# Experts of 112 token rows a pass in place of 128, with three passes behind the branch

## The reference

```python
def moe_swiglu(xn, w_router, w_gu, w_down):
    logits = (xn @ w_router).astype(jnp.float32)
    vals, idx = lax.top_k(logits, TOP_K)              # 2 of 8
    wts = jax.nn.softmax(vals, axis=-1)
    combine = jnp.sum(jax.nn.one_hot(idx, N_EXPERTS, dtype=jnp.float32) * wts[..., None], axis=-2).astype(xn.dtype)
    out = jnp.zeros_like(xn)
    for e in range(N_EXPERTS):
        out = out + combine[..., e:e + 1] * swiglu(xn, w_gu[e], w_down[e])
    return out
```

## Time and profile before

| | |
|---|---|
| median of 3 runs | 1527.17 us (1526.97 to 1527.71) |
| profiled execution, span from first to last instruction | 1525.5 us |
| mean granted TensorE clock | 0.996 |
| PE busy | 1492.0 us (98%) |
| PEld busy | 1214.1 us (80%) |
| DVE busy | 1187.4 us (78%) |
| ACT busy | 986.0 us (65%) |
| POOL busy | 57.1 us (4%) |
| DMA | 455.57 MB, mean 299 GB/s |

### The profile page before, as it was taken

The page is one execution under the profiler, slowest core; times in us unless marked ns, Lnnn a source line. Parts: engine busy times, 40 slices in busy tenths (PEclk is TensorE's granted clock), DMA queues, the critical chain, the costliest instruction groups (busy, mean ns, idle before and its releaser), DMA issues.

```text
span 1525.5 us, 20065 instructions
## 1 busy us (share of the span) xinstructions
PE 1492.0 (98%) x7081; PEld 1214.1 (80%) x7081; DVE 1187.4 (78%) x1047; ACT 986.0 (65%) x1001; POOL 57.1 (4%) x83
## 2 busy tenths in 40 slices
PE   7999999999999989999999999999999999999998
PEld 6888788887776568888888888888888888888886
DVE  1489655545658558898888889889888889888997
ACT  4645444444525527778777778778778778778774
POOL 2000100000111010000000000000000000000100
PEclk9999999999999989999999999999999999999999
DMA  9333585448638039999999999999999999999994
GB/s 363 130 111 111 185 257 180 178 166 220 217 138 290 15 110 374 369 363 386 394 367 377 394 378 363 393 391 355 395 376 362 395 385 357 393 392 356 397 392 169
DMA packets 213026, 455.57 MB, mean 299 GB/s; under 512 B 9857, under 2 KB 36522, under 8 KB 212970
## 3 DMA queue, kind: packets, MB, share of 16 engines
q1 hardware_dynamic: 206624, 441.48, 79.8%
q0 software_dynamic: 3536, 12.96, 2.1%
q10 hardware_dynamic: 2810, 0.40, 0.2%
HBM read 434.89 MB, written 19.92 MB: 298 GB/s over the span
## 4 chain that ended last, share of the span: by engine, by line
PE 94%; DVE 4%; POOL 1%; issue 1%; ACT 0%; DMA 0%; DVEq 0%; POOLq 0%; ACTq 0%
PE bank L2354 60%; PE bank L1947 8%; PE bank L1964 4%; PE bank L1817 4%; PE bank L1858 3%; PE bank L2033 2%; PE bank L2209 2%; PE bank L1839 2%; PE bank L2374 2%; PE bank L1891 1%; PE bank L2103 1%; PE bank L2067 1%; DVE small L1517 1%; PE bank L2151 1%; PE bank L2178 1%
## 5 line engine op out<-in xcount | busy, mean ns | idle before, releaser
L1676 DVE TENSOR_TENSOR w_lo<-ring,w_hi 128x2048 fp32r<-128x2048 f32 x333 | 756.4, 2290 | 104.6 <-ACT w_hi L1027 104.0
L1027 ACT ACTIVATE w_hi<-ring 128x2048 fp32r<-128x2048 f32 x333 | 638.0, 1920 | 168.8 <-PE bank L2354 168.6
L2354 PE MATMUL bank<-w_hi,x_hi 128*128 128x512 f32 x896 | 244.3, 394 | 0.7 <-DVE x_lo L1684 0.7
L2354 PE MATMUL bank<-w_hi,x_lo 128*128 128x512 f32 x896 | 240.0, 390 | 0.0
L2354 PE MATMUL bank<-w_lo,x_hi 128*128 128x512 f32 x896 | 239.7, 389 | 0.0
L2354 PEld LDWEIGHTS bank<-w_hi,x_lo 128*128 128x128 f32 x896 | 168.2, 188 | 35.9
L2354 PEld LDWEIGHTS bank<-w_lo,x_hi 128*128 128x128 f32 x896 | 168.2, 188 | 35.2
L2354 PEld LDWEIGHTS bank<-w_hi,x_hi 128*128 128x128 f32 x896 | 164.5, 188 | 32.3 <-issue 0.9
L1241 DVE TENSOR_TENSOR ring_lo<-ring,f_whi 128x1024 fp32r<-128x1024 f32 x66 | 80.6, 1225 | 75.5 <-ACT f_whi L817 75.5
L2354 PE MATMUL bank<-w_hi,t_hi 128*128 128x512 f32 x448 | 122.6, 395 | 0.0
L2354 PE MATMUL bank<-w_hi,t_lo 128*128 128x512 f32 x448 | 121.1, 392 | 0.0
(11 more groups left out here) (307 smaller groups left out, 1596.6 us busy)
## 6 DMA issues: line engine op xcount, KB each, us to landing
ring<-in_moe_w_gu SPq DMA_DIRECT2D x224, 1024.0 KB, 7.6
ring<-in_moe_w_down SPq DMA_DIRECT2D x112, 1024.0 KB, 8.1
ring<-in_ffn_w_gu SPq DMA_DIRECT2D x22, 1024.0 KB, 8.1
ring<-in_hgrn_w_in SPq DMA_DIRECT2D x16, 1024.0 KB, 15.2
ring<-in_ffn_w_down SPq DMA_DIRECT2D x10, 1024.0 KB, 6.3
x_rows<-arena SPq DMA_DIRECT2D x2, 4096.0 KB, 20.2
ring<-in_kv_w SPq DMA_DIRECT2D x6, 1024.0 KB, 6.3
ring<-in_hgrn_w_out SPq DMA_DIRECT2D x4, 1024.0 KB, 6.3
```

What stands on the lines that cost most here:

```text
L1027: act.activation(w_hi[s % PARTS][:, :], raw[:, s % RAWS, :], ACT.Copy).then_inc(hi_ready, 1)
L1676: dve.tensor_tensor(w_lo[s % PARTS][:, :], raw[:, s % RAWS, :], w_hi[s % PARTS][:, :].bitcast(F32), ALU.subtract).then_inc(lo_ready, 1)
L2354: last = mm(out_, x_[k], w[:, k, 512 * b:512 * b + 512], start=start and k == 0 and n == 0, stop=stop and k == HALF // width - 1 and n == 2)
```

## The change

`CAP = 112` takes the place of `P = 128` wherever a tile or a matmul has a token row of an expert as a partition or a column, and `PASSES = 3` passes cover 256 rows at most (3 x 112 = 336). The scratch has 336 rows an expert instead of 256. The branch is taken at more than 112 rows of an expert, and then two further passes run instead of one. The zero fill covers all 2688 rows of `x_rows` and 2 x 112 rows of each expert in `y_rows`, in six DMAs of SP's instead of four; the waits for it go to 96. The core of the diff:

```diff
-ROWS = 2 * P
+CAP, PASSES = 112, 3
+ROWS = PASSES * CAP
...
                 sp.dma_start(x_rows.rearrange("(n p) c -> p n c", p=P)[:, :, 512 * a:512 * a + 512],
-                             b_zero.unsqueeze(1).broadcast_to([P, 2 * NE, 512])).then_inc(x_zero, 16)
-                sp.dma_start(y_rows.rearrange("(n q p) c -> q p n c", q=2, p=P)[1, :, :, 512 * a:512 * a + 512],
-                             b_zero.unsqueeze(1).broadcast_to([P, NE, 512])).then_inc(x_zero, 16)
+                             b_zero.unsqueeze(1).broadcast_to([P, NE * ROWS // P, 512])).then_inc(x_zero, 16)
+                for q in range(1, PASSES):
+                    sp.dma_start(y_rows.rearrange("(n q p) c -> q p n c", q=PASSES, p=CAP)[q, :, :, 512 * a:512 * a + 512],
+                                 b_zero[0:CAP, :].unsqueeze(1).broadcast_to([CAP, NE, 512])).then_inc(x_zero, 16)
...
-            with sp.If(most > P):
-                all_experts(NE)
+            with sp.If(most > CAP):
+                for q in range(1, PASSES):
+                    all_experts(q * NE)
...
-                    pool.dma_start(m_xg, rows(x_rows, e + 1, q)).then_inc(x_full, 16)
+                    pool.dma_start(m_xg[0:CAP, :], rows(x_rows, e + 1, q)).then_inc(x_full, 16)
...
-                    last = act.activation(x_hi[:, k, :], bank[:, b, P * (k % 4):P * (k % 4) + P], ACT.Copy,
+                    last = act.activation(x_hi[:, k, 0:CAP], bank[:, b, P * (k % 4):P * (k % 4) + CAP], ACT.Copy,
...
-                act.activation(t_hi[:, c % 2, :, :], bank[:, 4, :], ACT.Copy).then_inc(t_hi_ok, 1)
+                act.activation(t_hi[:, c % 2, :, 0:CAP], bank[:, 4, :].rearrange("p (b t) -> p b t", b=4)[:, :, 0:CAP],
+                               ACT.Copy).then_inc(t_hi_ok, 1)
...
-            dve.wait_ge(x_zero, 64)
+            dve.wait_ge(x_zero, 96)
...
-                                  m_P[:, tb, :], start=tb == 0, stop=tb == 1)
+                                  m_P[:, tb, 0:CAP], start=tb == 0, stop=tb == 1)
...
-                    last = tp(bank[:, b, P * (k % 4):P * (k % 4) + P], m_xg[:, P * k:P * k + P], ident)
+                    last = tp(bank[:, b, P * (k % 4):P * (k % 4) + CAP], m_xg[0:CAP, P * k:P * k + P], ident[0:CAP, 0:CAP])
...
-                    product([bank[:, 2 * (c % 2) + up, :]], 2 * gu_item(c, up) + a, E,
-                            [x_hi[:, k, :] for k in ks], [x_lo[:, k, :] for k in ks], 512, a == 0, a == 1)
+                    product([bank[0:CAP, 2 * (c % 2) + up, :]], 2 * gu_item(c, up) + a, E,
+                            [x_hi[:, k, 0:CAP] for k in ks], [x_lo[:, k, 0:CAP] for k in ks], 512, a == 0, a == 1)
...
-                    last = tp(bank[:, 4, P * b:P * b + P], m_h[:, c % 2, P * b:P * b + P], ident)
+                    last = tp(bank[:, 4, P * b:P * b + CAP], m_h[0:CAP, c % 2, P * b:P * b + P], ident[0:CAP, 0:CAP])
...
-                    product([bank[:, 5, :], bank[:, 6, :]], 2 * down_item(c) + a, E,
-                            [t_hi[:, c % 2, b, :] for b in bs], [t_lo[:, c % 2, b, :] for b in bs], D,
+                    product([bank[0:CAP, 5, :], bank[0:CAP, 6, :]], 2 * down_item(c) + a, E,
+                            [t_hi[:, c % 2, b, 0:CAP] for b in bs], [t_lo[:, c % 2, b, 0:CAP] for b in bs], D,
```

More of the change, by code:

```diff
@@ L630, in rows @@
             def rows(block, e, q):
-                return block[bass.ds(e * ROWS + q * P, P), :]
+                return block[bass.ds(e * ROWS + q * CAP, CAP), :]
             def stored(e, E, q):
-                pool.wait_ge(y_ready, E + (2 + q))
-                pool.dma_start(rows(y_rows, e, q), m_y).then_inc(y_out, 16)
+                pool.wait_ge(y_ready, E + (2 + min(q, 1)))
+                pool.dma_start(rows(y_rows, e, q), m_y[0:CAP, :]).then_inc(y_out, 16)
             def brought():
@@ L650, in all_experts @@
                     pool.wait_ge(x_ps, 2 * E0)
-                    pool.dma_start(m_xg, rows(x_rows, 0, q)).then_inc(x_full, 16)
+                    pool.dma_start(m_xg[0:CAP, :], rows(x_rows, 0, q)).then_inc(x_full, 16)
                 with pool.Fori(0, NE - 1) as e:
@@ L659, in all_experts @@
                 pool.wait_ge(y_out, 16 * (E0 + NE))
-            pool.wait_ge(x_zero, 64)
+            pool.wait_ge(x_zero, 96)
             pool.wait_ge(y_out, 16)
@@ L674, in _ @@
             most = pool.value_load(flag[0:1, 0:1], min_val=0, max_val=T)
-            with pool.If(most > P):
-                all_experts(NE, 1)
+            with pool.If(most > CAP):
+                for q in range(1, PASSES):
+                    all_experts(q * NE, q)
                 pool.wait_ge(mixed, 1)
@@ L1050, in expert @@
                         act.wait_ge(e_h, E * NCH + (c - 1))
-                    act.activation(m_sl[:, c % 2, :], bank[:, 2 * (c % 2), :], ACT.Silu).then_inc(e_sl, 1)
+                    act.activation(m_sl[0:CAP, c % 2, :], bank[0:CAP, 2 * (c % 2), :], ACT.Silu).then_inc(e_sl, 1)
                     if c:
@@ L1056, in expert @@
                         act.wait_ge(PT_ps, 1)
-                        act.activation(m_PT[:, :], bank[:, 7, 0:T], ACT.Copy).then_inc(PT_ready, 1)
+                        act.activation(m_PT[0:CAP, :], bank[0:CAP, 7, 0:T], ACT.Copy).then_inc(PT_ready, 1)
                 split_to(min(2 * gu_item(NCH - 1, 1) + 1 + PARTS, HALVES + ahead), E)
@@ L1074, in expert @@
                             act.wait_ge(*used(HALVES - 1, E))
-                        act.activation(m_y[:, 512 * half:512 * half + 512], bank[:, 5 + half, :], ACT.Copy).then_inc(y_ready, 1)
+                        act.activation(m_y[0:CAP, 512 * half:512 * half + 512], bank[0:CAP, 5 + half, :], ACT.Copy).then_inc(y_ready, 1)
                 else:
-                    act.activation(m_y[:, :], bank[:, 5:7, :].rearrange("p b n -> p (b n)"), ACT.Copy).then_inc(y_ready, 1)
+                    act.activation(m_y[0:CAP, :], bank[0:CAP, 5:7, :].rearrange("p b n -> p (b n)"), ACT.Copy).then_inc(y_ready, 1)
                 splits[0] = ahead
@@ L1093, in _ @@
             most = act.value_load(flag[0:1, 0:1], min_val=0, max_val=T)
-            with act.If(most > P):
+            with act.If(most > CAP):
                 act.wait_ge(sc_ps, 4)
-                all_experts(NE, 1)
+                for q in range(1, PASSES):
+                    all_experts(q * NE, q)
         @block.vector
@@ L1763, in _ @@
             most = dve.value_load(flag[0:1, 0:1], min_val=0, max_val=T)
-            with dve.If(most > P):
+            with dve.If(most > CAP):
                 dve.memset(small[:, 505:506], 0.0).then_inc(mixed, 1)
-                all_experts(NE, 1)
+                for q in range(1, PASSES):
+                    all_experts(q * NE, q)
                 for tb in range(TB):
@@ L2441, in _ @@
             most = pe.value_load(flag[0:1, 0:1], min_val=0, max_val=T)
-            with pe.If(most > P):
-                all_experts(NE, 1)
+            with pe.If(most > CAP):
+                for q in range(1, PASSES):
+                    all_experts(q * NE, q)
 _INS = ["x", "norm_mix", "norm_ffn", "hgrn_w_in", "hgrn_w_out", "hgrn_g_norm", "kv_norm", "kv_w",
```

27 lines of the change are left out of this document (13 added, 14 removed).

## The result

The changed kernel takes 1549.28 us (median of 4 runs, 1548.69 to 1549.45) against 1527.18 for the kernel before on the same chip: a ratio of 1.0146, interval 1.0133 to 1.0158. It is slower by 22.1 us, where a gain of 3.8 us was forecast. The profiled execution has a span of 1547.8 us, against 1525.5 before.

The account below looks back on a forecast made before the run. PE was taken to bound the expert stage. Transposes -3.7 and first gather -0.1, all else zero, gave -3.8 us, so 1523.4 us; the forecast's own range was 1522.5 to 1525.3, the overall range 1516.5 to 1528.0.

Parts of the forecast that it names:

- What bounds the kernel, and the branch: Expert stage: PE sets the pace, DMA and DVE close behind; largest expert count 102 is below 112, so no extra pass.
- Zero fill: Scratch zeroing on SP's queue: 5.8 MB more at 384 GB/s takes 15 us, landing at 450.3; cost 0, bounds 0 and 2 us.
- the cover: Slack before the zero fill's landing delays DVE at line 1470: 1.8 us, and 3.3 us until the chain would move.
- rival E: Zero fill lands late enough to make the kernel slower; 3 us net needs 5.8 MB at 230 GB/s; chance 0.02.
- Products: The 4032 expert product matmuls: shorter load, 188 to 174 ns, gains zero; 6 us less or 2 us more allowed.
- the excess of 11 to 12 ns: Product pitch of 228 ns against 216 at line 1817, claimed to come from streaming 512 float32r columns, not the load.
- Transposes: 280 transposes in `turn` and `turn_x`: 16 fewer moving columns save 11.8 to 13.3 ns each, 3.7 us taken.
- First gather: First expert's `gather`, ACT copies and DVE subtractions on the chain once: 0.1 us less, from fewer elements.
- A: Expert products: the load is on the path after all, up to 27 us less, 1497 us; chance 0.04.
- B: Expert products: the matmul's excess goes with the columns, 6 us more gain, about 1517.5 us; chance 0.08.
- C: No change: transposes' pitch not set by moving columns, or zero fill eats 1 to 2 us; 1524.2 to 1527; chance 0.22.
- D: Expert products slower: float32r load loses a fast form below 128 columns and passes the pitch; 1563 us; chance 0.04.

## Why the prediction was wrong, point by point

**What bounds the kernel, and the branch.** Right: PE sets the pace of the expert stage in every one of these kernels, and the extra passes do not run.

**Zero fill: this is the step that failed.** The bytes were right (5.8 MB), and the sum with them comes out once all of them move from 128 partitions: 450.3 forecast, 448.8 measured (449.1 to 450.4 in the six other kernels with that fill). Mis-sized was the rate. "At 384 GB/s" came from DMAs with 128 partitions, and was applied to four DMAs that read from 112; those bring the last packet at 468.4 us. The working said that the cover would be gone at 320 GB/s (and slowed only the 5.8 MB that are new, while 7.3 MB changed their shape), and gave rival E, which names this very wait, 0.02, because all stretches with a full queue lay at 378 to 391. But no row of before has a DMA of another number of partitions, so these rows bound nothing for the new shape. For a transfer that the trace doesn't show, the bounds "0 and 2 us" were far too narrow. The price was 16.6 us at DVE's wait (468.72 - 452.14), and 2.8 us more that no term provided for: from DVE's first instruction of the attention to the first product it takes 117.3 us instead of 114.5. The half clock in 460 to 480 us lies there: four matmuls that take 0.88 us at full clock take 1.71. The other kernels with the wait need 117.2 (112 partitions in the other order), 116.9 (64 partitions) and 115.4 (the longer scratch alone), and none without it more than 114.5. No run has the wait without the half clock, so the rest of the 2.8 us is put down to it by argument.

**Products.** Right: the load is not on the path (174 ns as worked out, and 134 ns at 64 columns bring nothing). That "the excess of 11 to 12 ns belongs to the matmul itself" is neither contradicted nor shown: the length of the load has no part in it, but the load's columns change the pitch. Mis-sized was the upper allowance: "half a nanosecond, 2 us" for an unseen width; it measured 1.9 ns, 7.2 to 7.5 us. The excess of 11 to 12 ns over line 1817's pitch was seen, not understood, and then treated as independent of the columns.

**Transposes.** Right: 0.39 us for four, 3.5 us in total, 3.7 forecast. With the products wide and the fill from 128 partitions the kernel gains 3.4 us, 3.8 forecast.

**First gather, ACT, DVE, the rest.** Not contradicted; 0.1 us is too little to tell. From DVE's first instruction of the attention to the first product, six of the seven kernels with the repaired fill take 114.0 to 114.3 us, against 114.5 before, and the two kernels with the old gather and the old order (narrow products, split fill) take 114.0 and 114.3. The seventh, with the fill from 128 partitions alone, takes 113.3; its granted clock from 560 to 565 us was 0.77, where it was 0.60 before. The tail is within 1 us.

**The rivals.** A and B fell: the pitch rose. C fell too: the transposes gained, and the fill cost far more than 2 us. E occurred. (The "forecast's own range" up to 1525.3 doesn't follow from the terms given for it, transposes at 3.3 or 3.7 and the fill at 0 to 1: they reach 1524.8, from 1523.4.) D has its direction, slower products, but not its mechanism: the load stayed where it was forecast, 56 ns short of the pitch. The Trainium skill, page "TensorE: Matmul & The Clock Gate", section "Weight-path perf modes", speaks of 128 weights as the condition of a fast load; 188 ns at 128 against 187 at 127 shows no such step for float32r here, so the loss of 4.2 ns a product between these two is not that.

## What to carry to other kernels

A DMA's rate goes with its number of partitions in these runs: write zeros and other fill from all 128 and pick the piece size to match, and before counting a setup transfer as hidden, compare its landing, at the rate of its own shape, with the cover in us. Cut the moving side of a transpose where rows are unused (108.7 to 96.1 ns here), and leave the stationary side of float32r products in such a stream at 128 columns even if some are waste: of this change that gives 1523.77 us, 0.9976 of the kernel before (0.9965 to 0.9986). That quick mean is a finding of this stream and was measured in no other. A shape that the trace doesn't have needs a bound as wide as the nearest unlike rows allow, not as the like ones suggest.

## What the runs showed of the hardware

- The same 7.3 MB from 128, 112 and 64 partitions land at 448.8, 468.4 and 467.1 us. With 64 the DMA engines are all busy at 198 to 203 GB/s; with 112 they are all busy at 310 to 353 GB/s and then run out of work one after the other (shares 0.63, 0.06), until about one of the 16 is left.
- Products of 512 float32r columns have a pitch that depends on the number of stationary columns, not evenly: 227.5 ns at 128, 231.7 at 127, 229.8 at 112, 229.6 at 64. Single pitches differ within one width: 127 columns have stretches at 226 to 227 ns and at 233. Loads take 134 ns at 64 columns and 188 at 128, and their length has no part in it.
- In a wait of 13.2 us of PE in mid-kernel its granted clock fell to 0.50, and the next 10 us, with PE busy again, still stood at 0.55. Four matmuls of 0.88 us took 1.71 there.
